# Four modulation vectors of a two-layer block computed in other places of one kernel

## The reference, cut to what matters

```python
def ada_modulation(c, w, b):
    mod = jax.nn.silu(c) @ w + b
    shift, scale, gate = jnp.split(mod, 3, axis=-1)
    return shift[:, None, :], scale[:, None, :], gate[:, None, :]

for layer in range(DEPTH_2):
    g, mw, mb = mix_norms[layer]
    shift, scale, gate = ada_modulation(c, mw, mb)
    h = rms_norm(x, g) * (1.0 + scale) + shift
    mixer = rglru_mixer if layer % N_MIXERS == 0 else fox_mixer
    x = x + gate * mixer(h, *mixer_params[layer])
    g, mw, mb = ffn_norms[layer]
    shift, scale, gate = ada_modulation(c, mw, mb)
    h = rms_norm(x, g) * (1.0 + scale) + shift
    x = x + gate * peer_ffn(h, *peer_params[layer])
```

## Time and profile before

| | us |
|---|---|
| median of three runs | 2807.86 |
| lowest, highest | 2807.11, 2816.17 |
| the profiled execution: its time | 2813.6 |
| the profiled execution: its span | 2811.5 |
| busy PE, DVE, ACT, POOL | 2542.9, 1697.3, 1283.7, 1395.9 |
| mean granted clock of TensorE, of 2.4 GHz | 0.944 |

### The profile page before, as it was taken

How to read it: one execution, slowest core, us unless ns; L and a number is a source line. 1 busy time by engine, 2 the same in 40 slices (tenths; PEclk the granted TensorE clock), 3 DMA queues, 4 the chain that set the end, 5 groups by cost and what they waited for, 6 DMA issues and landing times.

```text
span 2811.5 us, 46246 instructions
## 1 busy us (share of the span) xinstructions
PE 2542.9 (90%) x17498; PEld 2342.0 (83%) x17498; DVE 1697.3 (60%) x2949; ACT 1283.7 (46%) x2140; POOL 1395.9 (50%) x569
## 2 busy tenths in 40 slices
PE   7968378988768999999999998979999999999998
PEld 7867378888768999999888887856899999988887
DVE  7247757922892695666555553465297566655555
ACT  4455524333454544444445454324545444445444
POOL 4779866773436798666200003623599666500000
PEclk9989589998888999999999999979999999999999
DMA  4467445764324555444566564411455444456664
GB/s 163 149 208 226 174 139 199 247 191 169 97 76 138 179 181 172 149 145 150 173 194 189 193 191 137 145 53 59 136 189 187 152 150 150 151 194 191 191 192 145
DMA packets 125333, 457.81 MB, mean 163 GB/s; under 512 B 13904, under 2 KB 14288, under 8 KB 124752
## 3 DMA queue, kind: packets, MB, share of 16 engines
q1 hardware_dynamic: 124848, 450.73, 49.8%
q10 hardware_dynamic: 288, 4.33, 0.4%
HBM read 453.95 MB, written 1.05 MB: 162 GB/s over the span
## 4 chain that ended last, share of the span: by engine, by line
PE 71%; DVE 11%; POOL 9%; issue 6%; ACT 2%; DMA 1%; POOLq 0%; DVEq 0%; SPq 0%; ACTq 0%
PE ms L1072 25%; PE mm L662 17%; PE mm L1034 17%; POOL low L1501 6%; PE ms L1054 4%; PE mm L669 3%; POOL mod_sums L1519 3%; DVE work L1552 2%; DVE work L1549 2%; PE mm L692 2%; DVE parts L1546 2%; PE mm L680 1%; DVE work L1546 1%; DVE parts L1591 1%; DMA ring<-w_ffn_up 1%
## 5 line engine op out<-in xcount | busy, mean ns | idle before, releaser
L1501 POOL TENSOR_TENSOR low<-ring,high 128x1024 fp32r<-128x1024 f32 (+1 forms) x502 | 1236.3, 2475 | 1021.7 <-ACT high L1194 842.2
L1398 ACT ACTIVATE high<-ring 128x1024 fp32r<-128x1024 f32 x506 | 535.7, 1059 | 349.0 <-PE ms L1072 348.1
L1034 PE MATMUL mm<-hs,high 128*128 128x256 f32 x4096 | 524.1, 281 | 3.4 <-ACT high L1194 3.4
L1072 PE MATMUL ms<-high,wts 128*128 128x512 f32 x2048 | 510.7, 392 | 0.0
L1034 PEld LDWEIGHTS mm<-hs,high 128*128 128x128 f32 x4096 | 490.1, 188 | 3.8 <-issue 3.8
L1990 DVE TENSOR_TENSOR low<-ring,high 128x1024 fp32r<-128x1024 f32 x256 | 313.4, 1226 | 293.9 <-ACT high L1398 293.9
L1072 PEld LDWEIGHTS ms<-high,wts 128*128 128x128 f32 x2048 | 384.5, 188 | 83.5
L1194 ACT ACTIVATE high<-ring 128x1024 fp32r<-128x1024 f32 (+1 forms) x252 | 258.8, 1031 | 236.8 <-PE mm L662 134.2
L662 PE MATMUL mm<-hs,high 128*128 128x256 f32 x2608 | 335.7, 282 | 17.6 <-DVE work L1549 11.9
L662 PEld LDWEIGHTS mm<-hs,high 128*128 128x128 f32 x2608 | 318.8, 192 | 20.7 <-issue 13.2
L1034 PE MATMUL mm<-hs,low 128*128 128x256 f32 x2048 | 278.5, 278 | 10.7 <-POOL low L1501 10.6
(11 more groups left out here) (268 smaller groups left out, 3047.5 us busy)
## 6 DMA issues: line engine op xcount, KB each, us to landing
ring<-w_peer_experts SPq DMA_DIRECT2D x512, 512.0 KB, 3.9
ring<-w_mod SPq DMA_DIRECT2D x72, 512.0 KB, 4.5
ring<-w_ffn_up SPq DMA_DIRECT2D x44, 512.0 KB, 4.4
ring<-w_peer_q SPq DMA_DIRECT2D x32, 512.0 KB, 3.4
ring<-w_last_mod SPq DMA_DIRECT2D x24, 512.0 KB, 4.3
ring<-w_lru_in SPq DMA_DIRECT2D x22, 512.0 KB, 3.4
ring<-w_gates SPq DMA_DIRECT2D x16, 512.0 KB, 3.4
ring<-w_ffn_down SPq DMA_DIRECT2D x16, 512.0 KB, 4.3
```

The lines of the kernel that those rows point to most:

```text
L1034: ins_ = pe.matmul(mm[:, s_ % BANKS, 0:T], w_[:, k * P:(k + 1) * P], hs[:, b_, k, :], start=pass_ == 0 and k == 0, stop=pass_ == 2 and k = ...
L1072: ins_ = pe.matmul(ms[:, 2 * c + half, :], wts[:, s_ % 3, b_, c * P:(c + 1) * P], v_[:, half * 512:(half + 1) * 512], start=s_ == 0 and pa ...
L1398: act.activation(high[:, (q0 + i) % CUT, :], ring[:, (t0 + i) % RAW, :], ACT.Copy) \
L1501: pool.tensor_tensor(low[0:rows, cut_slot, 0:width], ring[0:rows, raw_slot, 0:width], high[0:rows, cut_slot, 0:width].bitcast(F32), ALU.su ...
```

## The change

Only the place and the means of the four modulations change; their tiles, the values and all other stages stay.

- Nothing of them is left in the stage of the mixers: `scale_mods`, `add_mods`, `sum_mods`, the wait `mods_taken` and the two buffers `scaled` and `mod_sums` go.
- The first (`mod0`) takes the place of the fourth in the feed-forward layer, by the same code.
- The second (`mod1`, 24 tiles) is computed by PE from the ring itself: per tile eight fp32 products of 128 x 128 by one column of silu(c), summed in PSUM. The tiles stand around the norms: `(part 0, part 1)` are ahead of and behind the norm's own products, and eight stand between the LRU's gates and its way out. The look-ahead of ACT no longer crosses from one of these stages to the next (`RUN_END`), and ahead of three norms it cuts one tile instead of three.
- The third and fourth (`late_mods`, 48 tiles) are added up by DVE in the V products of the first expert layer, three tiles in eight steps, and summed by PE: one third of a modulation behind steps 30 and 51 each, four behind the last transposes, ahead of norm 6.

```diff
-            for name, count, width, parts__, cut in STREAM:
...
+            n = 0
+            while n < len(TILES):
+                name, i = TILES[n]
+                load_one(n)
+                n += 1
+                if name.endswith("experts") and i == RAW - 1:
+                    rounds = (KEYS if name == "peer0_experts" else 2 * KEYS) // RAW
...
+MOD1_AT = {"norm2": (1, 2), "norm3": (2, 2), "norm4": (2, 3), "lru_out": 8, "norm5": (1, 3)}
...
-_end = _q
+_end = _q - 1
 for _name, _count, _w, _p, _cut in reversed(STREAM):
     if _cut:
-        RUN_END[_name] = _end - 1
-    elif _name in ("mod", "ple", "peer0_keys", "peer1_keys"):
-        _end = min([CUT0[k] for k in CUT0 if TILE0[k] > TILE0[_name]])
+        RUN_END[_name] = _end
+        if _name in ("ple_gate", "lru_in", "lru_out", "peer0_q"):
+            _end = CUT0[_name] - 1
+    elif _name in ("ple", "peer0_keys", "peer1_keys"):
+        _end = min([CUT0[k] for k in CUT0 if TILE0[k] > TILE0[_name]]) - 1
...
                 dst_ = bank(n)[:, 0:T]
+                use_mods(f"norm{i}", 0)
                 for k in range(KD):
                     pe.wait_ge(sem("norm_squares"), KD * i + k + 1)
                     ins = pe.matmul(dst_, ones, hf[:, k, :], start=k == 0, stop=k == KD - 1)
                 S.did(ins, "outs")
+                use_mods(f"norm{i}", 1)
...
+            def use_mods(place_, part_):
+
+                if (place_, part_) == ("norm5", 0):
+                    pe.wait_ge(sem("mod1_taken"), 1)
+                for i in mods_at((place_, part_)):
+                    g, k = i // KD, i % KD
+                    w = slot(TILE_AT["mod1", i])
...
                     for j in range(KD):
...
+                        ins = pe.matmul(ms[:, 1, KD * g + j:KD * g + j + 1], w[:, j * P:(j + 1) * P], csilu[:, k:k + 1],
+                                        start=i == 0 and j == 0, stop=i == 23 and j == KD - 1, skip_group_check=True)
+                    ins.then_inc(sem("mod_tiles_used"), 1)
...
             lru_gates(RT - 2)
             lru_gates(RT - 1)
+            use_mods("lru_out", 0)
...
                     values(s_)
-
+                    if L == 0 and s_ in LATE_SUMS_AFTER:
+                        if s_ == LATE_SUMS_AFTER[0]:
+                            pe.wait_ge(sem("hidden_weighed"), KEYS - FIRST_MIXED)
+                        sum_late_mods([LATE_SUMS_AFTER.index(s_)], mm[:, 3])
...
+                if L == 0:
+                    sum_late_mods(range(2, 6), ms[:, 0])
...
-            ahead("ple_gate", 0)
+            ahead("ple_gate", 0, 0)
...
-            ahead("lru_in", 0)
+            ahead("lru_in", 0, 0)
...
-                ahead(f"peer{L}_q", 0)
+                ahead(f"peer{L}_q", 0, 2 if L else 0)
...
+                def add_late_mod(m):
+
+                    n, g, k = TILE_AT["late_mods", m], m // KD, m % KD
+                    tile_ready(dve, n)
+                    sums_ = late_sums[:, g % 4, :]
...
+                        ins = dve.scalar_tensor_tensor(out=sums_, in0=ring[:, n % RAW, :], scalar=csilu[:, k:k + 1],
+                                                       in1=sums_, op0=ALU.mult, op1=ALU.add)
```

More of the change, by code:

```diff
@@ L311, in tile_shape, with mods_at, late_mods_after, fill @@
             return rows, (P * DOWN[i % 3] if name == "ffn_down" else P * RECUR[i % 2] if name == "lru_out" else width)
+MOD1_AT = {"norm2": (1, 2), "norm3": (2, 2), "norm4": (2, 3), "lru_out": 8, "norm5": (1, 3)}
+def mods_at(place):
+    first = 0
+    for name, count in MOD1_AT.items():
+        for part, n in enumerate(count if isinstance(count, tuple) else (count,)):
+            if (name, part) == place:
+                return list(range(first, first + n))
+            first += n
+    return []
+def late_mods_after(s):
+    return list(range(s * LATE_MODS // KEYS, (s + 1) * LATE_MODS // KEYS))
 def stage_tiles(name, count):
-    if name == "last_mod":
+    own = [(name, i) for i in range(count)]
+    def fill(*places):
+        return [("mod1", i) for place in places for part in range(2) for i in mods_at((place, part))]
+    if name in ("mod0", "mod1", "late_mods"):
         return []
[L318 to L323, removed]
+    if name == "ffn_up":
+        order = []
+        for j in range(FFG):
+            order += [(name, 2 * j), (name, 2 * j + 1), ("mod0", j)]
+        return order + [("mod0", j) for j in range(FFG, 24)]
+    if name == "ple_gate":
+        return fill("norm2") + own
+    if name == "lru_in":
+        return fill("norm3", "norm4") + own
+    if name == "lru_out":
+        return fill("lru_out") + own
+    if name == "peer0_q":
+        return fill("norm5") + own
+    if name == "peer0_experts":
+        order = own[:KEYS]
+        for s in range(KEYS):
+            order += [own[KEYS + s]] + [("late_mods", i) for i in late_mods_after(s)]
+        return order
+    return own
 TILES = [tile for name, count, _, _, _ in STREAM for tile in stage_tiles(name, count)]
@@ L581, in _ @@
             sp_.dma_start(masks, consts[:, CON_KEPT:CONSTW]).then_inc(sem("masks_loaded"), 16)
-            for name, count, width, parts__, cut in STREAM:
[L583 to L611, removed]
-                    continue
-                for i in range(RAW):
-                    load_one(i)
-                what, value = raw_free(base)
-                with sp_.Fori(1, count // RAW) as r:
-                    for j in range(RAW):
-                        sp_.wait_ge(sem(what), r * RAW + (value + j - RAW))
-                        load(base + j, src[bass.ds(r * RAW + j, 1), :, :].rearrange("a p w -> (a p) w"))
@@ new lines, in load, with load_one @@
+            def load(n, which):
+                w = which.shape[-1]
+                sp_.dma_start(ring[:, n % RAW, 0:w], which).then_inc(sem(f"slot{n % RAW}_loaded"), 16)
+            def load_one(n):
+                name, i = TILES[n]
+                src = streams[name]
+                if n >= RAW:
+                    what, value = raw_free(n - RAW)
+                    sp_.wait_ge(sem(what), value)
+                if name == "ffn_down":
+                    m, a_ = i // 3, i % 3 * SLOT
+                    load(n, src[m][:, a_:a_ + P * DOWN[i % 3]])
+                elif name == "lru_out":
+                    m, a_ = i // 2, i % 2 * P * RECUR[0]
+                    load(n, src[m][:, a_:a_ + P * RECUR[i % 2]])
+                else:
+                    load(n, src[i])
@@ L956, in _ @@
             for t in range(2):
-                w = slot(TILE0["ple"] + t)
+                w = slot(TILE_AT["ple", t])
                 for b in range(4):
```

172 lines of the change are left out of this document (79 added, 93 removed).

## The result

| | us |
|---|---|
| changed kernel, median of seven runs | 2826.43 (2823.23 to 2835.06) |
| kernel before, seven runs on the same chip | 2816.17 (2807.11 to 2820.86) |
| ratio | 1.0048, 95% interval 1.0034 to 1.0062 |
| the changed kernel's profiled execution: time, span | 2824.6, 2822.8 |
| its mean granted clock of TensorE | 0.944 |

The change makes the kernel slower by 0.48%, some 13.5 us; the interval lies above 0.3%. The prediction was 2816.3 for a kernel before at 2807.9, a step of +8.4; the spans of the two profiled executions differ by 11.3. The seven runs of the kernel before have a median 8.3 us above that of the three runs in the table ahead, so steps are to be compared, not levels.

A forecast was written before the change was run, and what follows sets the result against it. In the recurrent mixers, POOL's adds slow DVE and hold ACT; the floor is DVE and PE in turn. Saving 47.2 us and adding 55.6 gives +8.4 on 2807.9, so 2816.3 us; range 2789 to 2837.

The forecast's parts named there:

- step of +8.4: Whole kernel: predicted net slowdown in us, taken from the profiled execution and applied to the median of 2807.9.
- likeliest case: Whole kernel: the forecast as computed, 2816.3 us with its own range 2804 to 2827, given chance 0.73.
- Mixers, -47.2: Recurrent mixers: removing scalings, adds and sums frees DVE and ACT from POOL, 47.2 us saved, ends 44 and 50.
- The tiles on PE: Second modulation's one-column products: 16 records 1.84 us, 48 records 8.09, each further one 0.213, as the clock falls.
- first rival: PE's modulation tiles: one-column products keep the clock up, cost 31 us, net -16, 2792 us; chance 0.08.
- The LRU's way out, +23.7: LRU's way out: ACT's look-ahead waits behind modulation tiles ahead of the Gelu, delaying DVE's products; 23.7 us lost.
- second rival: LRU's way out: ACT is not held by the look-ahead, 23.7 us less, 2793 us; chance 0.05.
- The look-ahead, +1.3: Norm 2: ACT cuts two tiles after the norm, so one DVE difference falls behind POOL; 1.3 us lost.
- V loop +3.7: First V products: DVE's adds are hidden, two sums on PE inside the loop cost 3.7 us.
- norm 6 +7.5: Ahead of norm 6: four sums on PE, 64 records, delay the norm's products in a fallen clock; 7.5 us lost.
- third rival: V loop becomes bound by its loads, 41 us more, 2857 us; chance 0.10, half in a partial form near 2837.
- Beyond the last tile, 0: Stages from the attention's first product to the end: predicted to change by 0 us.

The follow-up runs named there:

- gelu_first: Changed kernel with ACT's look-ahead to the LRU's way out moved from ahead of the Gelu to behind the recurrence's sixth cast; 0.9982 of the kernel before, -5.1 us.
- no_late: Changed kernel without the third and fourth modulation: their loads, DVE's adds and PE's sums are left out; 1.0021 of the kernel before, +5.9 us.
- early_tiles: gelu_first with the first two tiles of the LRU's way out ahead of the eight modulation tiles in the ring; 0.9968 of the kernel before, -9.0 us.
- small_adds: Kernel before with each of POOL's 63 adds working on 8 of the 1024 columns; 0.9877 of the kernel before, -34.6 us.
- one_product: Changed kernel with one of the eight products per second-modulation tile left, loads and ring unchanged; 0.9972 of the kernel before, -7.9 us.
- before_short: Kernel before with only ACT's look-ahead shortened as in the changed kernel, the modulations staying where they were; 1.0041 of the kernel before, +11.5 us.
- no_mod1: Changed kernel without the second modulation's loads and products, ACT's shortened look-ahead kept; 0.9921 of the kernel before, -22.3 us.
- no_mod1_ahead: no_mod1 with ACT's look-ahead of the kernel before at all four places; 0.9870 of the kernel before, -36.6 us.
- spread: early_tiles with 16 second-modulation tiles on PE, eight more on DVE, late sums moved into the V loop, three-tile look-ahead at norms 2 and 5; 0.9886, -32.1 us.

## Why the prediction was right, and where it was not

The sign, the order of size and the largest single term were right: faster mixers by a sum of small things, and nearly all of it handed back where PE's tiles stand in front of other work. Its likeliest case (2804 to 2827) holds the median of 2826.4, at its edge. The step of +8.4 lies 1.2 us below the interval of the ratio (+9.6 to +17.5), and +13.5 lies within the steps that the likeliest case spans (-4 to +19).

That the sum came out so near is in part luck. In the table 8.0 us more were saved than predicted (55.2 for 47.2) and 4.9 more given back (60.5 for 55.6), so that two misses of opposite sign leave +5.3; the medians say 13.5, and 5.9 of the profiled difference lie where nothing was predicted. The trace of the changed kernel is also a cheap one in the stages of the tiles: in gelu_first, no_late and early_tiles, whose code is the same from norm 2 to the LRU's gates and at norm 5, these stages together cost 25.0, 30.6 and 30.8 us, here 27.1. In no_late, with the same code at the LRU as well, the way to the recurrence costs 23.8 us, here 21.1.

- **Mixers, -47.2.** The mechanism is shown by small_adds: the same operations fall to 1.2, 1.67 and 1.92 us with POOL's adds alone taken away. The size was 2.6 us short in the stage itself. Two rows behind it were put at nothing. The 2.8 us in the branches come from the four outputs that PE makes while DVE normalizes (from 293.21 on, with DVE's gate at 312.54); the prediction named them, but counted them only up to the first gate. The 3.2 us in the feed-forward layer are no more than that stage differs by between kernels with the same code there (244.3 to 248.9 in the changed kernel, gelu_first, one_product and no_late), so the traces don't show that the change gained them.
- **The tiles on PE.** 0.213 us a record with the clock at 0.5, and a clock that falls on its way, hold: 1.84 for 16 records at norm 5, 22.3 for 128 at the LRU (25.1 by the prediction's prices; the clock stayed up longer, and in no_late and early_tiles it was 25.0 and 25.1). The first rival (one-column products keep the clock up) is out by the windows at 779 to 791. The Trainium skill (TensorE: Matmul & The Clock Gate, Part 1, What's actually happening) lets the clock follow how busy the engine is; here the engine's records leave no gap and the clock falls, so the measurement decides against that reading.
- **The LRU's way out, +23.7.** Measured 21.1, by the chain that was predicted, link by link. gelu_first takes 18.6 us away by moving one call (17.3 by the two traces, from the gates' end to the end of the way out). The second rival (ACT is not held) is out.
- **The look-ahead, +1.3: the term that was wrong.** The prediction gave to "ACT now cuts two tiles after the norm" 1.3 us, for one of DVE's differences behind POOL, at norm 2 alone, and took three cuts off norm 3 as a gain. The gain is there, but before_short measures the whole, with this gain in it, at 11.5 us. The failure is the count: two cuts of 2.4 us meet a chain of eight operations of DVE, two of which wait for a cut each, PE waits behind those, and its clock falls for the next product; and at norm 5 the low parts are slowed in the same way, which was not priced at all (7.48 for 3.26; PE waits 0.51 us for it in the changed kernel, 0.59 and 1.90 in before_short). The LRU's way in, which the prediction had as zero, lost 4.9 us for the same reason (6.3 in before_short, 6.4 in no_mod1, 1.1 in no_mod1_ahead): here are the timelines of POOL, DVE and PE of the changed kernel, with seven cuts without a pause beside DVE's convolution (three of its operations took 5.98 us before), for which PE's first gates wait:

```profile
688.31 17.31 POOL L1512 TENSOR_TENSOR low<-ring,high 128x1024 fp32r<-128x1024 f32 x7 [15.38 <-ACT high L1239]
...
690.90 7.59 DVE L1551 SCALAR_TENSOR_TENSOR work<-work,vec 128x256 f32<-128x256 f32 x3
...
706.48 3.66 PE L703 MATMUL mm<-work 128*128 128x256 f32 x8 [3.65 <-DVE work L1551]
```

  The places from norm 2 to norm 5, the LRU's way out aside, cost 7.9 + 7.3 + 11.9 = 27.1 us where 20.7 were predicted. With 11.5 to 14.3 for the look-ahead, the tiles' own part is 13 to 16 us by this trace (no_mod1's 35.8 less the LRU's 21.1 gives 14.7), and it had been priced at 19.4: one term too small, the others too large. This split is argued in part, since a figure of medians is taken from one of a single trace, and the same stages vary by 6 us between traces.
- **V loop +3.7, norm 6 +7.5.** Measured 3.7 and 6.9. The third rival (loads) is out: 260 GB/s where it asked whether 264 could be had, PE busy for 354.5 of 356 us. no_late shows that adds and loads cost nothing there.
- **Beyond the last tile, 0.** Measured 5.9, of which 5.5 lie between the attention's first product and norm 7, where no instruction was changed (the last section). Without the 5.9 the two spans differ by 5.4 us, less than the interval of the medians allows (9.6 to 17.5). So either this part stands in the medians too, or the changed kernel's other executions lose more in the stages of the tiles than its profiled one; the runs don't tell, since they list no clock by stage.

## What to carry to other kernels

Where two engines hold each other up, an instruction at a time, as POOL's adds and cuts did DVE's operations here, work moved off the one speeds up the other; but ask also which of its cuts now fall beside the other's chains, since here a look-ahead shortened by two tiles, at three norms and the LRU's way out, cost 11.5 us. Filler for an idle engine is not free where its data stand in the same queue and the same ring as the next stage's weights (one_product, with an eighth of the products, still took 14 us more than no_mod1), and an in-order program must not have a wait for those weights ahead of work that needs none: moving one such call gave back 18.6 us. Put fillers where the gap is long (the 30 us of the recurrence took 160 records for 4.3 us), and around short gaps no more than fit: spread, with six tiles at norms 2 to 4 instead of twelve and none at norm 5, lost nothing at norms 2 to 4 and 0.5 us at norm 5.

## What the runs showed of the hardware that was not expected

**The clock's way up comes at another moment in other traces, and that is worth 6 us.** In the attention PE starts again after a pause with the same products in every kernel. In the kernel before PE runs at 1.2 GHz for 17.5 us (from 1876.80 to 1894.27), in the changed kernel for 29.4 (from 1882.16 to 1911.52). Windows of 4 us on PE alone (us, busy us and count, PEclk, DMA share, GB/s), the kernel before first:

```profile
1884.00:1888.00 4.00, 4.00 (x10) 0.50 0.00 0
1892.00:1896.00 4.00, 4.00 (x16) 0.76 0.00 0
1896.00:1900.00 4.00, 4.00 (x21) 1.00 0.00 0
```
```profile
1890.00:1894.00 4.00, 4.00 (x11) 0.50 0.00 0
1906.00:1910.00 4.00, 4.00 (x11) 0.50 0.00 0
1910.00:1914.00 4.00, 4.00 (x17) 0.83 0.01 2
1914.00:1918.00 4.00, 4.00 (x21) 1.00 0.00 0
```

In the other kernels, all with the same attention, the rise came after 17.5 us (one_product, small_adds), 21.2 (no_late), 23.5 (no_mod1) and 29.4 (gelu_first, early_tiles, before_short, no_mod1_ahead, spread). The stretch from the restart to norm 7's products lasted 89.5 to 95.8 us with it. Up to the rise PE's records stand almost without a gap (29.34 of 29.50 us in the changed kernel). No kernel was traced twice, so that this is chance and not a matter of the kernel is argued: kernels with the same code up to the attention but for one call or a few tiles have either value, and the mean granted clock of one kernel differs from run to run (0.938 to 0.944 in the changed kernel's seven). The way down varies too: the 64 records behind norm 3 took 8.9 us in the changed kernel, 11.5 in no_late and in early_tiles, and all 384 took 57.3, 58.5, 63.7 and 67.3 us (changed kernel, gelu_first, no_late, early_tiles). The Trainium skill (TensorE: Matmul & The Clock Gate, Part 1, What's actually happening) says that the moment of the change differs from run to run, by half a microsecond either way. The traces agree that it differs, but it does so by 12 us here, and the measurement decides.

**Dense products have two rates at the full clock.** Sixteen records of 256 columns take 1.98 us in some stretches and 2.05 in others. In the kernel before the window 676 to 686 us has 91 records of PE and the window 736 to 746 has 87, PE busy for all 10.00 us and the granted clock 1.00 in both. Every one of the eleven traces has stretches of both, at other places in each; what sets them is open.

For a reader: two single profiles of kernels with such stages can differ by 5 to 10 us without any part of the change in it. A ledger by stage shows where, but its rows carry the same scatter, so a row of a few microseconds needs a second trace or an experiment of its own.
